# First attention of a two-block transformer: one unit for the 16 meta rows, values for every two units, projection blocks between the last units

## The reference

```python
q, k, v, qi, ki, wi = split(h @ w_in)          # 16 query heads, 4 key/value heads of 64
q, k = rope(rms_norm(q)), rope(rms_norm(k))    # the index queries and keys are rotated too
score = sum_h(w * relu(qi @ ki))               # chooses 64 keys for each row
score = where(causal, score, -inf)
_, idx = top_k(score, 64)
valid = idx <= qpos
s = einsum('qgrd,qkgd->qgrk', q_blk, k[idx]) * scale
p = softmax(where(valid, s, -inf))
o = einsum('qgrk,qkgd->qgrd', p, v[idx])
h = h + o @ w_out                              # the output projection, 1024 x 1024
```

## Time and profile before

| | us |
|---|---|
| median of 3 runs | 2339.61 (2337.88 to 2339.95) |
| profiled execution | 2340.55 |
| its span | 2338.8 |
| PE busy | 2075.5 (89%) |
| DVE busy | 1595.2 (68%) |
| ACT busy | 1115.9 (48%) |

### The profile page before, as it was taken

How to read it: one execution, slowest core, us unless ns; L and a number is a source line. 1 busy time by engine, 2 the same in 40 slices (tenths; PEclk the granted TensorE clock), 3 DMA queues, 4 the chain that set the end, 5 groups by cost and what they waited for, 6 DMA issues and landing times.

```text
span 2338.8 us, 28200 instructions
## 1 busy us (share of the span) xinstructions
PE 2075.5 (89%) x9734; PEld 1332.0 (57%) x9734; DVE 1595.2 (68%) x3700; ACT 1115.9 (48%) x2730; POOL 643.7 (28%) x624
## 2 busy tenths in 40 slices
PE   7789998999999989887788988998998899888876
PEld 6769998778999987543223443443444444233322
DVE  5836677756778869767667476756749656676654
ACT  5445534545543445444445365543547445445543
POOL 0000010100001006544443233333324334444342
PEclk9899999999999998999999999999999999999999
DMA  6205586842679647999999999999999999999996
GB/s 235 91 28 180 173 322 234 291 151 82 215 243 358 221 152 290 407 419 420 420 420 420 421 415 419 399 421 420 411 422 410 415 421 419 420 420 410 417 420 288
DMA packets 131348, 768.22 MB, mean 328 GB/s; under 512 B 14480, under 2 KB 16272, under 8 KB 59280
## 3 DMA queue, kind: packets, MB, share of 16 engines
q0 software_dynamic: 87552, 587.24, 61.6%
q1 hardware_dynamic: 42944, 177.81, 21.2%
q10 hardware_dynamic: 720, 1.51, 0.2%
HBM read 765.45 MB, written 1.05 MB: 328 GB/s over the span
## 4 chain that ended last, share of the span: by engine, by line
PE 53%; DMA 29%; DVE 10%; ACT 4%; issue 3%; POOL 1%; SPq 0%; ACTq 0%; DVEq 0%; POOLq 0%
DMA arena<-experts,arena 28%; PE bank L974 14%; PE bank L561 9%; PE bank L563 9%; PE bank L562 9%; PE bank L1009 6%; DVE arena L2376 3%; PE bank L698 1%; PE bank L677 1%; POOL arena L527 1%; DMA alibi<-ada_w 1%; ACT arena L1523 1%; PE bank L663 1%; ACT arena L1522 1%; DVE arena L1893 1%
## 5 line engine op out<-in xcount | busy, mean ns | idle before, releaser
L974 PE MATMUL bank<-arena 128*128 128x512 f32 x2048 | 987.2, 622 | 163.9 <-ACT arena L1523 163.7
L2376 DVE CUSTOM_DVE_ANT_0 arena<-arena 128x1024 f32<-128x1024 f32 x512 | 633.4, 1239 | 461.6 <-DMA arena<-experts,arena 460.9
L974 PEld LDWEIGHTS bank<-arena 128*128 128x128 f32 x2048 | 379.2, 196 | 723.9 <-issue 367.2
L527 POOL DMA_INDIRECT arena<-experts,arena x512 | 559.8, 1093 | 834.0 <-PE bank L974 788.9
L1518 ACT ACTIVATE arena<-arena 128x1 f32<-128x1 f32 x512 | 103.3, 202 | 589.9 <-DVE arena L2376 587.8
L1237 ACT CAST whi<-wring 128x1024 fp32r<-128x1024 f32 x228 | 238.0, 1049 | 253.4 <-PE bank L563 245.9
L1783 DVE TENSOR_TENSOR wlo<-wring,whi 128x1024 fp32r<-128x1024 f32 x216 | 263.3, 1224 | 112.4 <-ACT whi L1237 112.0
L1523 ACT ACTIVATE arena<-tab,arena 128x128 f32<-128x128 f32 x512 | 205.5, 401 | 16.7
L513 POOL DMA_DIRECT2D arena<-ada_w x64 | 34.0, 532 | 637.3 <-DVE adaM L1830 619.0
L561 PE MATMUL bank<-hTh,whi 128*128 128x256 f32 (+2 forms) x584 | 173.5, 297 | 16.1 <-DVE hTl L1792 9.6
L563 PE MATMUL bank<-hTh,wlo 128*128 128x256 f32 (+2 forms) x584 | 168.1, 288 | 0.0
(11 more groups left out here) (330 smaller groups left out, 2997.5 us busy)
## 6 DMA issues: line engine op xcount, KB each, us to landing
wring<-w_stream SPq DMA_DIRECT2D x236, 512.0 KB, 4.0
wring<-w_stream SPq DMA_DIRECT2D x48, 1024.0 KB, 9.0
arena<-ada_w POOLq DMA_DIRECT2D x64, 512.0 KB, 5.3
alibi<-ada_w POOLq DMA_DIRECT2D x32, 512.0 KB, 5.7
arena<-experts,arena POOLq DMA_INDIRECT x512, 14.9
xT<-xT_in SPq DMA_DIRECT2D x1, 1088.0 KB, 5.1
alibi<-alibi_in ACTq DMA_DIRECT2D x1, 1024.0 KB, 4.9
tab<-tab_in SPq DMA_DIRECT2D x1, 831.0 KB, 6.6
```

Source lines behind the costliest of these rows:

```text
L527: pool.indirect_dma_start(g_ring[:, r], None, experts[n // (2 * PEER_HEADS)], bass.IndirectOffsetOnAxis(idx[:, s // SLOTS % 2, s % SLOTS:s ...
L974: last = mm(banks[2 * t + b][:, :], diag[:, r], g_ring[:, r, D + b * TILE_N:D + (b + 1) * TILE_N], start=s % SLOTS == 0, stop=s % SLOTS == ...
L2376: v.tensor_tensor_reduce(g_ring[:, r, 0:D], g_ring[:, r, 0:D], hrow[:, t], 1.0, 0.0, ALU.mult, ALU.add, act8[:, r:r + 1]).then_inc(dot_don ...
```

## The change

The meta rows become one unit of their own ahead of the loop. Their 16 heads are laid over 128 partitions (four heads by 32 rows, four times 16 columns), scored by 32 small matmuls into banks 4 to 7, and masked, exponentiated and scaled by one short series of instructions; PE transposes them at n = 0 and multiplies the values at n = 1. To have the query scale in that layout, `pair_sums` writes the sums of the meta rows to all four groups of 32 partitions. The loop then has eight units instead of twelve, and the first four turns do two choosing rounds each. `values_a` is called after every second unit, for the heads of half h, with 128 columns per matmul and `par` innermost. The projection's blocks with even kc need only half 0: two chunks' even blocks are placed ahead of the last value group, two behind it, then the odd blocks. The table of constants has 16 columns `meta` in place of 128 columns `zeros`.

```diff
--- before.py
+++ after.py
-        quads = [[(r, x) for r in range(3) for x in range(4)], [(r, x) for r in (1, 2) for x in range(4)]]
+        quads = [[(r, x) for r in (1, 2) for x in range(4)], [(r, x) for r in (1, 2) for x in range(4)]]
...
-            return 2 * quads[0][n][0] + 1 if layer == 0 else 6 + n
+            r, x = quads[layer][n]
+            return 5 + n if layer else 1 + 2 * (r - 1) + x // 2
...
-                def values_a(r):
-                    nq = ROWS[r][1]
-                    for u in range(2):
-                        if r or u:
-
-                            pe.wait_ge(ot_copied, 2 * r + u)
+                def values_a(n):
+                    r, x = quads[0][n]
+                    h, nq = x // 2, ROWS[r][1]
+                    pe.wait_ge(ot_copied, outs(0, n))
+                    rhs = ptA[r].rearrange("p k (g h a) q -> p k g h a q", g=4, h=2)
+                    for g in range(4):
+                        for kt in range(r + 1):
+                            nk = key_tile(r, kt)[1]
+                            for par in range(2):
+                                last = mm(banks[7][64 * par:64 * par + 64, P * g:P * g + nq], vA[0:nk, kt, g * HD:(g + 1) * HD],
+                                          rhs[0:nk, kt, g, h, par, 0:nq], start=kt == 0, stop=kt == r)
+                    last.then_inc(pv_done, 1)
+
+                def meta_scores():
+                    for x in range(4):
+                        for half in range(2):
+                            for b in range(4):
+                                g = slice(32 * b, 32 * b + 32)
+                                last = mm(banks[4 + b][g, N_META * x:N_META * (x + 1)], qA[g, 2 * x + half, 0:32],
+                                          kA[g, half, 0:N_META], start=half == 0, stop=half == 1)
+                                if x == 3 and half == 1:
+                                    last.then_inc(s_done, 1)
+
+                def meta_turn():
+                    pe.wait_ge(p_scaled, 1)
+                    for x in range(4):
+                        last = nc.tensor.transpose(banks[6][0:N_META, P * x:P * (x + 1)], m_s[:, x], ident)
+                    last.then_inc(pt_done, 1)
+
+                def meta_values():
+                    pe.wait_ge(pt_copied, 1)
+                    rhs = ptA[0].rearrange("p k (g h a) q -> p k g a h q", g=4, h=2)
+                    dst = banks[7][:, 0:8 * N_META].rearrange("p (g h q) -> p g h q", g=4, h=2)
+                    for g in range(4):
                         for par in range(2):
-                            dst = banks[7][64 * par:64 * par + 64, :].rearrange("p (u h q) -> p u h q", u=2, h=2)
-                            for g in (2 * u, 2 * u + 1):
-                                for kt in range(r + 1):
-                                    nk = key_tile(r, kt)[1]
-                                    rhs = ptA[r].rearrange("p k (g h a) q -> p k g a h q", g=4, h=2)[0:nk, kt, g, par, :, 0:nq]
-                                    last = mm(dst[:, g % 2, :, 0:nq], vA[0:nk, kt, g * HD:(g + 1) * HD], rhs, start=kt == 0,
-                                              stop=kt == r)
-                        last.then_inc(pv_done, 1)
+                            last = mm(dst[64 * par:64 * par + 64, g], vA[0:N_META, 0, g * HD:(g + 1) * HD],
+                                      rhs[0:N_META, 0, g, par], start=True, stop=True)
+                    last.then_inc(pv_done, 1)
 
                 def values_b(n):
...
+                if layer == 0:
+                    meta_scores()
                 for n in range(N + 3):
                     if n < N:
                         scores(n)
+                    if layer == 0 and n == 0:
+                        meta_turn()
+                    elif layer == 0 and n == 1:
+                        meta_values()
                     if 2 <= n < N + 2:
                         turn(n - 2)
                     if n >= 3:
                         copied(n - 3)
                         if layer:
                             values_b(n - 3)
-                        elif quads[0][n - 3][1] == 3:
-                            values_a(quads[0][n - 3][0])
+                        elif quads[0][n - 3][1] % 2:
+                            values_a(n - 3)
                     yield
...
+            def whole_part(g, c, first, step):
+
+                for kc in range(first, KC, step):
+                    last = mm(banks[c][:, 0:T], wring[:, g % 2, c, kc], hT[:, kc], start=kc == 0, stop=kc == KC - 1)
+                if kc == KC - 1:
+                    last.then_inc(lin_done, 1)
...
-                            last = mm(banks[4][0:nq, 4 * r:4 * r + 4], sq_pair[:, n % 2, half, q0:q0 + nq], heads,
-                                      start=half == 0, stop=half == 1)
+                            for dst, queries in ([(slice(0, P), slice(q0, q0 + nq))] if r else
+                                                 [(slice(32 * b, 32 * b + 32), slice(0, 32)) for b in range(4)]):
+                                last = mm(banks[4][dst, 4 * r:4 * r + 4], sq_pair[:, n % 2, half, queries], heads,
+                                          start=half == 0, stop=half == 1)
...
-            for _ in attention(0):
-                pass
-            pe.wait_ge(ot_copied, 6)
-            out_proj(G_AOUT, T, None, 0)
+            units = attention(0)
+            for n in range(N_QUADS[0] + 2):
+                next(units)
+            pe.wait_ge(sm_done, 4 * N_QUADS[0])
+            pe.wait_ge(ot_copied, 4)
+            for c in range(2):
+                pe.wait_ge(w_landed[G_AOUT % 2][c], 16 * (G_AOUT // 2 + 1))
+                whole_part(G_AOUT, c, 0, 2)
+            next(units)
+            for c in range(2, CPT):
+                pe.wait_ge(w_landed[G_AOUT % 2][c], 16 * (G_AOUT // 2 + 1))
+                whole_part(G_AOUT, c, 0, 2)
+            pe.wait_ge(ot_copied, 5)
+            for c in range(CPT):
+                whole_part(G_AOUT, c, 1, 2)
+            for c in range(CPT):
+                pe.wait_ge(res_done, c + 1)
+                pe.wait_ge(w_landed[(G_AOUT + 1) % 2][c], 16 * ((G_AOUT + 1) // 2 + 1))
+                whole_part(G_AOUT + 1, c, 0, 1)
             mlp(0, 0)
...
+                if layer == 0:
+                    act.wait_ge(nmx_done, 1)
+                    af(m_s, m_s, ACT.Exp).then_inc(exp_done, 1)
...
+                    if layer == 0 and n == 0:
+                        act.wait_ge(pt_done, 1)
+                        src = banks[6][0:N_META, :].rearrange("p (x g q) -> p x g q", x=4, g=4)[:, :, :, 0:N_META]
+                        nc.scalar.copy(ptA[0].rearrange("p k (g x) q -> p k x g q", g=4)[0:N_META, 0], src).then_inc(pt_copied, 1)
+                    elif layer == 0 and n == 1:
+                        act.wait_ge(pv_done, 1)
+                        src = banks[7][:, 0:8 * N_META].rearrange("p (c q) -> p c q", c=KC)
+                        nc.scalar.copy(hT[:, :, 0:N_META], src).then_inc(ot_copied, 1)
...
+                def meta_masked():
+                    for b in range(4):
+                        g = slice(32 * b, 32 * b + 32)
+                        dve.wait_ge(s_done, b + 1)
+                        mark(v.tensor_tensor(m_s[g], banks[4 + b][g, 0:4 * N_META].rearrange("p (x k) -> p x k", x=4),
+                                             table("meta")[g].unsqueeze(1).to_broadcast([32, 4, N_META]), ALU.add))
+                    settle()
+                    link(v.tensor_reduce(m_mx, m_s, AX.X, ALU.max))
+                    link(v.tensor_tensor(m_s, m_s, m_mx.unsqueeze(2).to_broadcast(rows_of), ALU.subtract))
+                    v.tensor_tensor(m_s, m_s, m_scale.unsqueeze(2).to_broadcast(rows_of), ALU.mult).then_inc(nmx_done, 1)
+
+                def meta_scaled():
+                    dve.wait_ge(exp_done, 1)
+                    link(v.tensor_reduce(m_sum, m_s, AX.X, ALU.add))
+                    link(v.reciprocal(m_rs, m_sum))
+                    v.tensor_tensor(m_s, m_s, m_rs.unsqueeze(2).to_broadcast(rows_of), ALU.mult).then_inc(p_scaled, 1)
+
+                if layer == 0:
+                    meta_masked()
...
                         masked(n)
+                    if layer == 0 and n == 0:
+                        meta_scaled()
                     if layer and n >= 4:
                         out_lo(n - 4)
                     if 1 <= n < N + 1:
                         scaled(n - 1)
                     if 2 <= n < N + 2:
                         turned(n - 2)
-                    if layer == 0 and n < 7:
+                    if layer == 0 and n < 4:
                         select_round(2)
-                        if n == 6:
-                            select_round(2)
+                        select_round(2)
+                        if n == 3:
                             keys_selected(2)
...
+            own = table("block32").rearrange("p (b c) -> p b c", b=4)[:, :, 0]
```

(3 more changed lines are left out.)

47 lines of the change are left out of this document (15 added, 32 removed).

## The result

| | before | after |
|---|---|---|
| median of the runs, us | 2338.74 (2336.09 to 2339.95) | 2319.91 (2317.44 to 2322.11) |
| profiled execution, its span | 2340.55, 2338.8 | 2322.11, 2320.3 |
| granted clock, mean | 0.969 | 0.975 |
| first product of the MLP begins | 190.2 | 174.6 |
| first expert gather issued | 902.2 | 885.9 |

The ratio is 0.992, with an interval of 0.9908 to 0.9932: 18.8 us less. The forecast was 2326.0, a gain of 13.5 us. The new time lies inside the range for 8 in 10, 0.4 us above its lower end, and outside the forecast's own range of 2321 to 2331.

What follows compares the result with a forecast made beforehand. No engine is full in the first attention: DVE paces its beginning, a chain across engines its end. Last mask 8.6 earlier + 5.8 after it - 0.9 = 13.5 us gain, to 2326.1; 8-in-10 range 2319.5 to 2334.5.

Steps and rivals of the forecast that it cites:

- Before the attention: Ahead of the first attention: 12 extra pair-sum records cost 1.0 us, less 0.1 for the shorter table load; net +0.9.
- Meta scores: First attention's start: 64 PE records take 1.7 us, there at 98.5, and DVE waits 0.8 us that nothing hides.
- Turn of a unit with two rounds: Loop over 144-key units on DVE: one turn with two choosing rounds takes 3.15 + 1.01 = 4.16 us.
- Last mask: Last 272-key unit of the first attention: its mask starts at 131.5 instead of 140.12, 8.6 us earlier.
- Value groups: First attention's value products on PE: alternating halves overlap, so 32 records take 2.0 us and 48 take 2.85.
- The clock's +1.2: After PE's 3 us idle before 136.3: 1.2 us added for the lowered clock, moving 142.4 to 143.6.
- The rival of halves in a row: Value groups: halves run one after the other, 3.5 and 5.2 us; gain only 5.8, time 2333.8; chance 0.12.
- Draining at each alternation: Value groups: array empties at each of 80 matmuls, 27 us more, time 2353; the slower rival, chance 0.04.
- Two chunks' blocks: Output projection: 16 even-block records, 3.7 us, stand before the last value group; the remaining projection takes 25.9.
- its 2.3: First attention's end: 2.3 us of copy waits (0.97, 0.66, 0.67), now covered by transposes and projection blocks.
- From the last rotation to the projection's end: First attention, from last rotation to the projection's last record: 79.5 us instead of 94.
- more goes than I think: From 117 to 133 only DVE paces, and the clock stays up: gain 19 us, time 2320.5; chance 0.08.

Runs made afterwards that it cites:

- the kernel before with the short table: Kernel before the change, only with unused zero columns of the constant table cut from 128 to 16; measured 2335.24 us, ratio 0.9984.
- the kernel with values alone: Kernel before the change, twelve units kept, but values of 128 columns with alternating halves computed after every second unit; measured 2330.21 us, ratio 0.9963.

## Why the prediction was right, step by step

The mechanism was right in the attention, which is 15.6 of the 18.5 us between the two profiles. The sum of its terms fell 2.1 us short there, and the other 3 us were no part of it. The attention's gain alone would have given some 2323 us (an estimate: 2338.74 less 15.6), inside the forecast's own range. With the other 3 us the time lies outside that and just inside the wider one. That it came so near the 2320.5 of a rival is luck, as the end of this section shows.

- **Before the attention: +0.9 was forecast, 0.0 came.** The step that failed was the price of the 12 extra pair-sum records. The 24 records took 1.29 us where 12 had taken 1.17 to 1.24: they overlap even more than the lower bound (0.2 for 12) said. Rotation ended at 96.5 instead of 97.5; before it was 96.6. Since this point moves between 95.8 and 96.8 over all the profiles, 0.0 is known to about half a microsecond.
- **Meta scores.** 64 records took 0.73 us, not 1.7, so DVE did not wait the 0.8 us. The four meta masks took 0.97 instead of 0.64, and DVE waited 0.57 us for the second unit's scores at 103.74, which had not been counted. The misses cancel, and the key mask came at 117.2 as worked out (118 with the 0.9). The Trainium skill, TensorEngine Tiling (Array Packing), Instruction Overhead, prices a matmul at about 60 cycles. The prediction made 3.2 us of it, at the lower clock and with a matmul for each record. The granted clock in these records was 1.00, and two records are one matmul of the code, so the estimate by the page is 1.6 us if it means records and 0.8 if it means matmuls of the code. The 0.73 us measured is 11 ns for a record and 23 for a matmul; the trace agrees with the second count and cannot say which is meant. Key Properties on the same page of the Trainium skill says that tiles operate independently. The trace agrees: 64 records of about 178 ns each lie within 0.73 us.
- **Turn of a unit with two rounds:** 4.16 forecast, 4.17 measured.
- **Last mask:** 131.5 forecast (without the 0.9), 130.47 measured. The first value group ended at 119.1 instead of 120.5 (at 119.7 in the second profile of this kernel), since PE's clock was already at its upper level from 117 on (1.00 in the second stretch), and unit 5 was masked at 120.26 instead of 122.
- **Value groups:** 2.0 and 2.85 forecast; 1.97, 1.97 and 2.84 measured at full clock, 3.27 behind the idle time. The clock's +1.2 was 1.16 + 0.43 = 1.6 in this profile, and 1.3 to 2.8 in others. The rival of halves in a row had priced a group of 48 at 5.2; in a row it took 5.08, so its price was right and its condition was not met. Draining at each alternation would have shown as 27 us more; the groups leave no room for it.
- **Two chunks' blocks:** 3.7 and 25.9 forecast, 3.83 and 25.93 measured. Their worth, 1.7 to 1.9 us, is mostly the two waits that the prediction named among its 2.3.
- **From the last rotation to the projection's end:** 79.5 forecast, 78.5 measured (96.5 to 175.0).
- **From the MLP on, every stage of its old length:** this failed. "The table of constants is 57 KB shorter" was priced at 0.1 by its load. What it does to the time is to move the buffers behind it, the gathers' ring among them, by 448 bytes, worth 3.5 us (0.9984, 0.9975 to 0.9993) by the kernel before with the short table. The forecast had looked at the transfer only and not at what the allocation behind it does.

The rival "more goes than I think" named 2320.5, close to the 2319.9 that came. Of its mechanism little was seen: the earlier start of the scores gave 1.0 us, and the clock behind the last mask cost more than forecast, not less. Its time was met mostly through the ring's place and the 0.9 that was not spent.

What stays open: which address counts, and why. Three places were tried, and multiples of 32 that are none of 64 gave two different times (1403 to 1406, and 1407 to 1409). Whether 64, 128 or 256 would give what 512 gives was not tried, nor a multiple of 512 that is none of 1024. Nor is it settled why single runs at one place spread by 2 to 3 us in the gathers, or why the stretch from the MLP's start to the first gather takes from 709.5 to 713.8 us over all the profiles; the 0.7 us gained there in the profiled pair lies within that spread.

## What to carry to other kernels

Before a change is judged by a fraction of a per cent, look at what it moves in SBUF: a table, a spare column or a pad ahead of a buffer that large transfers land in shifts that buffer, and should be an experiment of its own, or be held fixed. Where a kernel waits for DMA, try the place of the destination of its large rows early, beginning with a multiple of 512 or 1024 bytes; here 160 bytes of padding gave 18 us, as much as the whole change. Where products fill only half of the array's columns, let neighbouring instructions alternate between the halves: the order of the loops alone made 48 records 1.8 times as fast.

## What the runs showed of the hardware

- The place of a DMA's destination in SBUF changes its rate, with the same source, the same number of packets and the same size: 512 gathers took 1387 us at one multiple of 512 bytes and 1403 to 1409 at two odd multiples of 32. Transfers from DRAM into SBUF went on at 423 GB/s on average for 1.2 ms, at 426 to 428 in most slices.
- Products on different tiles of the array overlap far below the duration of one: 64 records of 32 rows, 32 columns of weights and 16 moving columns in 0.73 us at a granted clock of 1.00, 11 ns each, where one lasts 178 ns.
- Two column halves run side by side only where neighbouring instructions alternate: 48 records in 2.84 us so, in 5.08 with 24 of one half and then 24 of the other.
- An idle time of 3.43 us on PE cost 1.6 us more in what followed, by the granted clock: 12 transposes in 2.69 us instead of 1.53, 48 value records in 3.27 instead of 2.84. In other runs the cost after the same idle time was 1.3 to 2.8 us. After an idle time of 1.84 us the same records kept 1.50 and 2.84. After one of 2.11 us, in the kernel with values alone, 12 transposes took 2.30 and 32 value records 2.79 instead of 1.97.
